# Splitting the weights of the MLP two units at a time in a float32 transformer block

## What is computed

```python
h = h + (g_mla * y_mla + g_fox * y_fox) @ w_out[l]
hn = rmsnorm(h, mlp_norm[l])
u = jnp.square(jax.nn.relu(hn @ w_up[l]))
h = h + u @ w_down[l]
return rmsnorm(h, final_norm)
```

## Time and profile before

| what | value |
|---|---|
| time of the kernel, median of 3 runs | 1278.83 us (1278.75 to 1278.84) |
| span of the profiled execution | 1278.0 us |
| PE busy | 1269.1 us (99%) |
| DVE busy | 763.0 us (60%) |
| ACT busy | 597.0 us (47%) |
| POOL busy | 137.6 us (11%) |
| granted PE clock | full speed in all 40 slices |

### The profile page before, as it was taken

How to read it: one execution, slowest core, us unless ns; L and a number is a source line. 1 busy time by engine, 2 the same in 40 slices (tenths; PEclk the granted TensorE clock), 3 DMA queues, 4 the chain that set the end, 5 groups by cost and what they waited for, 6 DMA issues and landing times.

```text
span 1278.0 us, 14326 instructions
## 1 busy us (share of the span) xinstructions
PE 1269.1 (99%) x5666; PEld 1053.4 (82%) x5666; DVE 763.0 (60%) x767; ACT 597.0 (47%) x690; POOL 137.6 (11%) x239
## 2 busy tenths in 40 slices
PE   9999999999999999999999999999999999999997
PEld 7888888888888888888888888888888888888886
DVE  6676566646676677566665655444455656554544
ACT  6655345444555444444454544333344444453443
POOL 0122001103221111110111110000000101100000
PEclk9999999999999999999999999999999999999999
DMA  9698856756887688787778686555667777856563
GB/s 334 245 296 276 259 180 212 232 184 198 252 281 213 203 293 281 231 252 231 248 229 265 216 261 199 196 193 192 194 221 235 235 247 232 287 171 215 196 193 120
DMA packets 83139, 293.88 MB, mean 230 GB/s; under 512 B 11320, under 2 KB 12416, under 8 KB 82432
## 3 DMA queue, kind: packets, MB, share of 16 engines
q1 hardware_dynamic: 67536, 243.04, 57.9%
q0 software_dynamic: 14528, 48.00, 12.9%
q10 hardware_dynamic: 1008, 1.92, 0.4%
HBM read 269.45 MB, written 23.47 MB: 229 GB/s over the span
## 4 chain that ended last, share of the span: by engine, by line
PE 94%; DMA 2%; DVE 1%; POOL 1%; ACT 1%; issue 1%; DVEq 0%; POOLq 0%; ACTq 0%
PE bank L604 91%; DMA turn_rows<-blocks 1%; DMA kn<-turn_rows 1%; DVE hl L1044 1%; DMA turned_h<-turn_rows 1%; PE bank L705 1%; PE bank L687 0%; PE bank L685 0%; POOL query_rows L523 0%; PE bank L729 0%; PE bank L708 0%; POOL query_rows L522 0%; DVE blocks L1179 0%; POOL rope_t L521 0%; ACT gate L869 0%
## 5 line engine op out<-in xcount | busy, mean ns | idle before, releaser
L1044 DVE TENSOR_TENSOR hl<-raw,hl 128x1024 fp32r<-128x1024 f32 x451 | 550.3, 1230 | 467.1 <-ACT hl L824 466.7
L824 ACT ACTIVATE hl<-raw 128x1024 fp32r<-128x1024 f32 x451 | 475.4, 1059 | 599.2 <-PE bank L604 564.7
L604 PE MATMUL bank<-hl,hn_hl 128*128 128x512 f32 x1536 | 348.5, 389 | 0.0
L604 PE MATMUL bank<-hl,u_hl 128*128 128x512 f32 x1536 | 348.5, 389 | 0.0
L604 PE MATMUL bank<-hl,x_hl 128*128 128x512 f32 (+1 forms) x1536 | 345.3, 386 | 0.0
L604 PEld LDWEIGHTS bank<-hl,hn_hl 128*128 128x128 f32 x1536 | 288.3, 188 | 59.9
L604 PEld LDWEIGHTS bank<-hl,u_hl 128*128 128x128 f32 x1536 | 288.3, 188 | 59.9
L604 PEld LDWEIGHTS bank<-hl,x_hl 128*128 128x128 f32 x1536 | 283.9, 188 | 57.4 <-DVE hl L1035 0.7
L604 PE MATMUL bank<-hl,m_hl 128*128 128x512 f32 x384 | 87.2, 389 | 0.0
L604 PEld LDWEIGHTS bank<-hl,m_hl 128*128 128x128 f32 x384 | 72.1, 188 | 15.0
L500 POOL DMA_DIRECT2D turn_rows<-blocks x35 | 19.7, 562 | 555.2 <-DVE blocks L1179 554.2
(11 more groups left out here) (152 smaller groups left out, 451.8 us busy)
## 6 DMA issues: line engine op xcount, KB each, us to landing
raw<-weights SPq DMA_DIRECT2D x454, 512.0 KB, 4.3
turn_rows<-blocks POOLq DMA_DIRECT2D x34, 512.0 KB, 3.6
turned<-turn_rows POOLq DMA_DIRECT2D x96, 128.0 KB, 5.2
prob_rows<-prob_blocks POOLq DMA_DIRECT2D x8, 384.0 KB, 2.8
prob_t<-prob_rows POOLq DMA_DIRECT2D x32, 96.0 KB, 5.8
turned_h<-turn_rows POOLq DMA_DIRECT2D x20, 128.0 KB, 5.1
x_rows<-x_n POOLq DMA_DIRECT2D x2, 1024.0 KB, 8.3
resid<-x_n POOLq DMA_DIRECT2D x1, 2048.0 KB, 10.7
```

The source lines that it names most:

```text
L604: return nc.tensor.matmul(bank[:, gr.pair + tb, 0:gr.cols], tile[:, k, x_part, tb * P:tb * P + P], w, start=k == 0 and not x_part and not ...
L824: nc.scalar.activation(hl[:, slot, 0], raw[:, slot], ACT.Copy).then_inc(unit_hi, 1)
L1044: nc.vector.tensor_tensor(hl[:, slot, 1], raw[:, slot], hl[:, slot, 0].bitcast(F32), ALU.subtract).then_inc(unit_split, 1)
```

## The change

A constant is added: from unit 200 on (the first unit of the up projection), ACT and DVE make the high and low parts at odd units alone, for that unit and the one before, each by one operation over two neighbouring slots of the ring (128 x 2048). The semaphores are raised by 2 at its end. At even units nothing but the wait for `unit_used` is left on ACT and nothing at all on DVE. PE's program, SyncE's program, POOL's program and the lists of due work are the same as before.

```diff
+TWO_BY_TWO = 200
...
+                if u >= TWO_BY_TWO:
+                    if u % 2:
+                        act.wait_ge(unit_loaded[slot - 1], loaded)
+                        act.wait_ge(unit_loaded[slot], loaded)
+                        nc.scalar.activation(hl[:, slot - 1:slot + 1, 0], raw[:, slot - 1:slot + 1],
+                                             ACT.Copy).then_inc(unit_hi, 2)
+                    return
                 act.wait_ge(unit_loaded[slot], loaded)
                 nc.scalar.activation(hl[:, slot, 0], raw[:, slot], ACT.Copy).then_inc(unit_hi, 1)
...
+                if u >= TWO_BY_TWO:
+                    if u % 2:
+                        dve.wait_ge(unit_hi, u + 1)
+                        nc.vector.tensor_tensor(hl[:, slot - 1:slot + 1, 1], raw[:, slot - 1:slot + 1],
+                                                hl[:, slot - 1:slot + 1, 0].bitcast(F32),
+                                                ALU.subtract).then_inc(unit_split, 2)
+                    return
                 dve.wait_ge(unit_hi, u + 1)
                 nc.vector.tensor_tensor(hl[:, slot, 1], raw[:, slot], hl[:, slot, 0].bitcast(F32),
```

## The result

The change makes the kernel slower: 1298.24 us median (1297.65 to 1300.36, 4 runs) against 1278.84 (1278.75 to 1278.95). The ratio is 1.0152, 95% interval [1.0137, 1.0167]: +19.4 us, or 1.5%, where 1285.2 was forecast and 1297 was the upper end of the range. The direction was right, the size three times too small.

The account below looks back on a forecast made before the run. PE was taken to bound the kernel, with no idle time to give back; stalls of 1.66 + 0.7 + 2.23 + 1.42 + 0.33 = 6.3 us raised the 1278.0 span to 1284.3, median 1285.2 us, range 1282 to 1297.

Parts of the forecast that it names:

- What bounds the kernel, and the distances: PE, busy 99% of the span, sets the end; each low part has 5.4 us of slack, which the change spends.
- F: The time at which PE starts a unit, and so has freed the ring slot of the unit before.
- The cost of the long operations: 2048-column operations continued straight from 512 and 1024 columns: ACT 1.92 us, DVE 2.31 us.
- Items 1, 3 and 4 (squares): PE stalls behind ACT's wait to square the residual: 1.66 us at 204, 2.23 at 412, 0.71 each at 428 and 444.
- Ends of up groups ... I cost that at nothing: At 13 group ends, 0.36 us slack and no engine stall; moved transfers priced at nothing, at most 0.9 us each.
- steady state: Pair ready at F + 4.46, slack 0.70 us, no stall; paired loads have 6.6 us to land, against 5.6 traced.
- Rival 1: Loads collide with turned-row reads, pair (11, 12) lands late, all 13 up-group ends stall 0.9 us: +12, 1297 us; chance 0.15.
- Item 2: Loads for units 208 and 209, issued among reads of turned rows, land late: 0.7 us stall (0 to 2.4).
- Item 5: Pair (396, 397) waits for a load behind the 1 MB of gain rows: 0.33 us stall (0 to 1.5).

Follow-up runs that it names:

- quiet_pairs: Changed kernel with the long operations on both engines only in units 280 to 327; 1278.93 us, 1.0 against the kernel before.
- six_slots: Changed kernel with six load slots instead of four from unit 200 on, each pair loaded one pair earlier; 1289.12 us, 1.0084 against the kernel before.

## Why the prediction was wrong

The stalls in this execution come to 12.2 us more than the forecast: 4.1 at the ends of up groups, 3.0 at units 394 to 400, 2.1 at the last four units, 1.6 from the clock, 0.5 at unit 216, and 0.9 in the slower first units and at unit 208.

**What bounds the kernel, and the distances:** right. PE sets the end, and a pair ready at F + 4.5 leaves 0.7 us. In the quiet stretches nothing stalls (`quiet_pairs`).

**The cost of the long operations:** right to 0.02 us.

**Items 1, 3 and 4 (squares):** right, 5.9 us against 5.3; the difference is PE's first unit after each stall, which takes 0.1 to 0.2 us longer. I gave that nothing.

**"Ends of up groups ... I cost that at nothing":** this failed. I had the loads for units 9 and 10 go out two us before the reads, and compared no landing with what was left. At unit 232 they go out at 653.2 and 653.6, between the store and the reads; ACT wanted them at 659.2, 6.0 us after the first issue, and could have had them 0.7 later without a stall; the second landed at 660.9, 7.7 us after the first issue. The 6.6 us of my steady state hold for the quiet stretches alone: at an end the low part before is later. The ends cost 4.1 us here, and 3.5 to 6.5 in the three other executions with four slots and long operations on both engines, at different ends each time. `six_slots` shows that late loads are the cause: with earlier loads all of it goes.

**Rival 1** had the place and the cause in kind (landings among turned rows), but with the wrong pair, 11 and 12, and with a stall at all 13 ends. That its 1297 us lie near the 1298.24 measured is luck: it had 12 us at the ends, where 4.1 were found. The rule of the Trainium skill that it named (SBUF — State Buffer, section SBUF: two separate sides) had no part: the reads were issued in 2.18 us beside a long operation of DVE. I had also stretched it. That a GpSimd which writes descriptors is locked out, the section states for operations of DVE in a two-port mode; for one with two inputs in SBUF, as the low part is, it names the lock "only against a GpSimd op that reads SBUF". The traces agree with that: the four issues show no hold, before or after.

**Item 2** (0.7, measured 1.0) came out near, and 0.9 without the stall ahead of it.

**Item 5** was mis-sized in the profiled execution. For unit 396 it had 0.33 us, and 1.65 were measured: I had ACT begin the pair (396, 397) 6.67 us after PE's start of unit 392, and it began after 9.0. In two other executions with the same gain rows it began after 7.1 and 7.4, with a step of 0.3 and 0.2, inside my 0 to 1.5. With the neighbours 394 and 400 it was 3.30 here and 0.7 and 1.6 in those two. I had priced single landings, not the loop of load, high part, low part and next load, in which each late low part sends the next loads out later, into the next reads.

**The last four units, missed:** 2.1 us. The order of `last_group` stood in my description of the kernel ("with the same waits"). PE takes half of 452 and half of 453 first, so it wants unit 454 at F + 2.72, not at F + 5.44; 4.46 + 0.28 - 2.72 = 2.02 could have been worked out, and 1.97 were measured, without the slower first unit.

**The bank at unit 216, missed:** 0.5 us. After two groups side by side PE wants the first one's banks again two units after it ends (unit 213); VectorE reads them only behind a pair, until 620.53, and PE starts then:

```profile
619.32 1.21 DVE L1270 TENSOR_TENSOR full<-full,bank 128x1024 f32<-128x1024 f32 x1
...
620.59 2.79 PE L605 MATMUL bank<-hl,hn_hl 128*128 128x512 f32 x11 [0.22 <-DVE full L1270]
```

**The clock, missed:** 1.6 us in this execution. Among the profiles of the other kernels with such stalls it fell not at all in two and twice in one.

**What remains open:** which ends of up groups stall in an execution, what the gain rows cost by themselves, whether the store or the reads hold the loads up, and what decides whether the clock falls behind a stall of about 2 us.

## What to carry to other kernels

Merging the operations that fill a ring saves their fixed part and doubles the grain of the ring: count what a slot has left between ready and wanted before and after, at every place where due work, an in-order wait or another order of use stands in the queue. Two neighbouring operations on two engines overlap, one merged pair of them does not (3.4 against 4.3 us here), so merging lengthens the path even where it shortens the work. If the engine that sets the end has no idle time, less work on the others gains nothing.

## What the runs showed of the hardware

- Ten stalls in seven profiles set PE's start back by 1.97 to 2.22 us, by the starts of the same product. Behind six of them the granted clock fell to 0.5 for 3.4 us (0.50 and 0.51 in the rows above), at a cost of 1.6 us; it began to do so 0.2 to 1.5 us after PE's restart. Behind four it stayed at full speed: three of 1.97 us and one of 2.22, the size behind which it fell three times. Behind stalls up to 1.88 us it never fell.
- PE's first unit after a stall, at full clock, took 2.82 to 2.89 us instead of 2.72.
- Two loads of 512 KB issued 0.4 us apart, between a store and reads of the same size, landed after 3.8 and 7.3 us.
- A subtraction of DVE took 0.69, 1.23 and 2.29 us for 512, 1024 and 2048 columns, a copy of ACT 0.63, 1.06 and 1.92 us: on both engines the straight line through the first two gives the third to within 0.02 us.
